# Layer 1 projections of a hybrid decoder step: the pages of cached keys are dealt to the units by kind, with weights 6, 3, 6, 6

## What is computed

```python
proj = _rmsnorm(x, norm_g) @ w_in                       # 1024 -> 4 * 1024 + 16
q, k, v, g, f = jnp.split(proj, [C_WIDTH, 2 * C_WIDTH, 3 * C_WIDTH, 4 * C_WIDTH], axis=-1)
q = _rmsnorm(q.reshape(Bn, L, C_HEADS, C_HEAD_DIM), q_g)
k = _rmsnorm(k.reshape(Bn, L, C_HEADS, C_HEAD_DIM), k_g)
v = v.reshape(Bn, L, C_HEADS, C_HEAD_DIM)
...
past_k = cache_k[page_table].reshape(Bs, -1, C_HEADS, C_HEAD_DIM)
...
s = jnp.einsum('bqhd,bkhd->bhqk', q, k_all).astype(jnp.float32) * ATTN_SCALE
```

## Time and profile before

| | us |
|---|---|
| median of 3 runs | 3198.45 |
| the runs | 3194.75 to 3200.6 |
| the profiled execution | 3206.94 |
| span of its instructions | 3205.4 |

### The profile page before, as it was taken

The page is one execution under the profiler, slowest core; times in us unless marked ns, Lnnn a source line. Parts: engine busy times, 40 slices in busy tenths (PEclk is TensorE's granted clock), DMA queues, the critical chain, the costliest instruction groups (busy, mean ns, idle before and its releaser), DMA issues. The chain is left out here.

```text
span 3205.4 us, 46935 instructions
## 1 busy us (share of the span) xinstructions
PE 2827.6 (88%) x17133; PEld 2246.4 (70%) x17133; DVE 1608.6 (50%) x2154; ACT 1024.0 (32%) x1721; POOL 1381.3 (43%) x986
## 2 busy tenths in 40 slices
PE   3887979695998999889999965999999999999999
PEld 2887868683774998879899963555555555554787
DVE  4222223234365678888555536455555555553432
ACT  4323132322245222212112211444454544544100
POOL 0000000001000477667888853777777777777000
PEclk9998989897998999989999986999999999999899
DMA  4101010104563688879777756977878878874532
GB/s 122 35 21 40 20 40 20 40 13 147 175 184 117 195 263 280 257 256 292 256 255 238 255 172 145 251 206 224 240 218 224 238 209 235 227 217 131 179 118 74
DMA packets 327904, 547.51 MB, mean 171 GB/s; under 512 B 76093, under 2 KB 220129, under 8 KB 319212
## 3 DMA queue, kind: packets, MB, share of 16 engines
q1 hardware_dynamic: 263564, 471.12, 50.0%
q10 hardware_dynamic: 61120, 58.83, 5.3%
q0 software_dynamic: 3008, 14.81, 1.3%
HBM read 449.58 MB, written 95.12 MB: 170 GB/s over the span
## 5 line engine op out<-in xcount | busy, mean ns | idle before, releaser
L1151 POOL TENSOR_TENSOR p_kp<-p_kp,p_qb 128x1024 f32<-128x1024 f32 x256 | 628.6, 2483 | 391.6 <-DMA p_kp<-in_cache_k_dram 313.3
L1997 POOL TENSOR_TENSOR at_acc<-at_acc,at_w 128x512 f32<-128x512 f32 (+3 forms) x576 | 644.8, 1119 | 231.1 <-ACT at_w L2125 165.4
L112 PE MATMUL p_pb<-p_w,x_xh 128*128 128x256 f32 x2048 | 595.0, 291 | 14.3 <-DVE p_w L1465 14.3
L2160 DVE TENSOR_REDUCE at_mx<-at_mx 128x1 f32<-128x512 f32 (+3 forms) x640 | 382.5, 608 | 425.7 <-PE at_mx L2032 312.0
L113 PE MATMUL p_pb<-p_w,x_xh 128*128 128x256 f32 x2048 | 582.3, 284 | 0.0
L114 PE MATMUL p_pb<-p_w,x_xl 128*128 128x256 f32 x2048 | 581.6, 284 | 0.0
L2125 ACT ACTIVATE at_w<-at_st,c_nckt 128x512 f32<-128x512 f32 (+3 forms) x640 | 389.5, 622 | 365.8 <-PE at_st L2058 193.4
L1567 DVE TENSOR_REDUCE p_sc<-p_kp 128x16 f32<-128x1024 f32 x256 | 308.2, 1215 | 230.6 <-POOL p_kp L1151 230.5
L112 PEld LDWEIGHTS p_pb<-p_w,x_xh 128*128 128x128 f32 x2048 | 393.6, 192 | 26.7 <-DVE p_w L1465 15.4
L113 PEld LDWEIGHTS p_pb<-p_w,x_xh 128*128 128x128 f32 x2048 | 395.5, 193 | 0.0
L114 PEld LDWEIGHTS p_pb<-p_w,x_xl 128*128 128x128 f32 x2048 | 394.6, 193 | 0.0
(11 more groups left out here) (296 smaller groups left out, 3837.2 us busy)
## 6 DMA issues: line engine op xcount, KB each, us to landing
p_kp<-in_cache_k_dram SPq DMA_DIRECT2D x256, 512.0 KB, 4.9
at_vp<-in_cache_v_dram SPq DMA_DIRECT2D x256, 512.0 KB, 5.4
o_mt<-mixed SPq DMA_DIRECT2D x32, 512.0 KB, 4.9
p_raw<-in_w_in_dram SPq DMA_DIRECT2D x32, 512.0 KB, 7.3
at_q<-qh SPq DMA_DIRECT2D x32, 512.0 KB, 10.7
at_k<-kh SPq DMA_DIRECT2D x32, 512.0 KB, 8.3
l_raw<-in_w_in_dram SPq DMA_DIRECT2D x20, 512.0 KB
mixed<-l_w POOLq DMA_DIRECT2D x8, 1028.0 KB, 4.2
```

What stands on the lines that cost most here:

```text
L112: nc.tensor.matmul(out, lhs[0], rhs[0], start=(k == 0), stop=False)
L1151: nc.gpsimd.tensor_tensor(kp[:, g % 4], kp[:, g % 4], qb[:], ALU.mult).then_inc(kmul, 1)
L1997: nc.gpsimd.tensor_tensor(t[:, 512 - wd:512], t[:, 512 - wd:512], W[n % RW][:, 0:wd], ALU.add).then_inc(accd, 1)
L2160: nc.vector.reduce_max(mx[:, u % 2, j, seg:seg + 1], MX[r % 2][:, 0:wd], AX.X).then_inc(mread, 1)
```

## The change

`keys_of` no longer deals the pages evenly. Each unit from 7 to 125 gets a weight by its kind, 6 for queries, values and gates and 3 for keys, and unit m gets the pages between the floors of the running sums' shares of 256. The first seven and the last two units still get none. Nothing else is changed; a keys unit now has one page or two, the others two or three.

```diff
     PAGES = B * z.PG
     FIRST = 7
+    SHARE = {"q": 6, "k": 3, "v": 6, "g": 6}
 
     def keys_of(m):
 
-        span = N - 2 - FIRST
-        lo, hi = ((max(0, min(span, x - FIRST)) * PAGES) // span for x in (m, m + 1))
+        share = [0] * FIRST + [SHARE[kind] for _, _, kind in UNITS[FIRST:N - 2]] + [0, 0]
+        lo, hi = (sum(share[0:x]) * PAGES // sum(share) for x in (m, m + 1))
         return range(lo, hi)
```

## The result

The changed kernel takes 3217.5 us in the median of 5 runs (3213.4 to 3220.0), against 3200.6 for the kernel before in the same comparison (5 runs, 3194.8 to 3205.0): a ratio of 1.0051, 95% interval 1.0037 to 1.0065, slower by some 17 us. Its profiled execution took 3217.5 us, like its median.

What follows compares the result with a forecast made beforehand. VectorE's queue was taken to pace the keys, the page loop values and gates; +12 - 45 + 52 - 11 = +8 us made 3215 us profiled, 3206.5 on the median's scale, range 3189 to 3223.

Steps and rivals of the forecast that it cites:

- Step A: Queries: nine more pages, between VectorE's sums alone (+5 us) and the page loop's pace (+14); taken as +12.
- Step B: Keys: 31 page sums fewer on VectorE and a shorter key gain, -45 us (-59 to -34).
- rival 1: Faster: queries' loop has room, VectorE drops below TensorE's pace in the keys; -13 us, 3185 us; chance 0.15.
- Step C: Values and gates: 21 more pages, each on the path at 2.5 us, +52 us (50 to 55).
- Rival 3: Added pages in values and gates hide behind the matmuls, only the keys' gain is left; -33 us, 3165 us; chance 0.05.
- Step D: Stage end: pages end last, so the stage closes some 7 us behind the last sum, not 18.5; -11 us.
- Rival 2: Clearly slower: keys' removed sums only uncover the VectorE-ScalarE chain, keys shrink by 34 only; +24 us, 3222 us; chance 0.12.
- Rival 4: No change: queries near their low end, keys a few us better, otherwise as forecast; -4 to +6 us; chance 0.28.
- three signs of being wrong: Values-and-gates page under 2.4 us; keys down to TensorE's pace; queries taking nine pages for nothing.

Runs made afterwards that it cites:

- the half product: Changed kernel, but GpSimd multiplies only half of each page's columns, so half the scores are left out: 3144.7 us, ratio 0.9831 to the kernel before.

## Why the prediction was right in its sign and half in its size

The forecast was +8 us, in a range of -9 to +25 against 3198.45; measured were +17. It came out toward the upper end of the +7 to +19 that the prediction gave its own steps. The direction and the mechanism hold; the size hangs in part on errors that cancelled. By its steps:

**Step A, queries, +12 forecast, +19 to +21 measured.** This is the term that was mis-sized most. The stretch from the earlier trace rows was right as a pace, but not what I made of it. The pages' tile before and after the one reload in the queries:

```profile
1088.00:1175.00 87.00, 0.00 (x0) 0.00 (x0) 37.48 (x32) 68.77 (x28) 1.00 0.84 276
1190.00:1268.00 78.00, 0.00 (x0) 0.00 (x0) 34.91 (x29) 70.74 (x30) 0.92 0.86 280
```

After the reload 29 pages took 78 us, 2.7 each as in the earlier trace rows. Before it the first four took their 9 us and the other 28 some 79, 2.8 each, because the loop starts empty: the fifth page's load can be issued only after the first sum. The reload held 11 us more, not 10. And I had taken 12 where the working gave 14, leaning towards VectorE as the bound; the half product shows that the loop was it. The range for the last query page, 1256 to 1265 us, missed 1268.

**Step B, keys, -45 forecast, -41 to -46 measured.** Right to a few us. VectorE's busy time came as described: 36 us of sums fewer and the gain at 1.10 us instead of 1.28, to 176 us where the working had 180. Its idle time of 32 us did not, and that the total of 29 was near it is luck: the waits for pages, reloads among them, fell to 14 us where the working had 24, and the waits for squares rose to 15 where it took 2 (in the second profile the two are 15 and 11 us). What I had not seen is that VectorE, once its arrears were made up, falls below TensorE's pace, so that the keys turn from VectorE's bound to TensorE's (200 busy of 208). That was rival 1's condition, and it came true without its gain, probably because the queries had left VectorE 20 us late (no run tests this alone).

**Step C, values and gates, +52 forecast, +45 to +48 measured.** Right in kind, 4 to 7 us too high: 21 pages at 2.1 to 2.3 us. The lower bound of 50 was too high, since two of the 155 pages lay multiplied when the stretch began: GpSimd has 153 products in it, 19 more than before and not 21, and is busy 371 us instead of 329. Idle it was 62 us instead of 56. Rival 3 is out by this.

**Step D, the close, -11 forecast, -7 to -13 measured.** The size is right, its reason only half: the pages do not end last. The last weights' low part,

```profile
1853.27 2.27 DVE L1466 TENSOR_TENSOR p_w<-p_raw,p_w 128x1024 fp32r<-128x1024 f32 x1
```

was followed by 54 us of pages, as worked out, but the gate rows' last store, issued at 1911.3, landed as the last, just as before: 3.65 us lie between that issue and the close in both profiles, while scores that end last close 3.7 us after the last sum, which would have been 1912.9. TensorE's last chunk began at 1858, some 2.5 us behind the low part, since its wait for the raw weights a unit earlier had put it back too. It was a tie that I decided for the wrong side, at 2 us.

The terms from the first profile of each kernel sum to 19 - 45 + 48 - 13 = 9 us, near the forecast's 8. That closeness is luck: 7 us too few in A stand against 4 too many in C and 2 too few saved in D. And that profile of before stood 6 to 9 us above its median, and I carried its difference over to after as if it were an offset of all profiles. It was not: after's profile stood at its own median. The rest of the miss lies there. The second profiles give +17 for the same four terms, with A at 21, B at -41, C at 45 and D at -7.

Of the rivals, none ended as the outcome. Rival 2 asked for keys that shrink by only 34; they did not. Rival 4, no change, is shut out by the interval. Of the prediction's own three signs of being wrong two came: a page in values and gates cost less than 2.4 us, and the keys came down to TensorE's pace. The scores' store was not the last of the stage either. What did come as written are the gain near 1.1 us, the 134 waits for products and TensorE's idling at the weights.

## What to carry to other kernels

Where a side loop (load, product, sum, slot freed) runs beside a main one, work out its own time for the whole stage first: as an estimate from the rows here, 252 pages at 2.6 us and seven reloads at 10 are 725 us, and what is left to the 801 of the three stretches before is idle time that a dealing can only move. Taking its work out of the stretch that looks worst then only makes the loop idle there, and the pages return at the loop's price, 2.1 to 2.3 us, where they had cost 1.3 to 1.7. What paid was to shorten the loop itself: the query row issued one wait earlier (-14 us), then the idle ends (a start at unit 3, more pages behind the last weights), some 36 us together.

Take a second profile, and the medians of several runs, before a term of a few us is read from the first: the same program's keys took 254 and 250 us, its close 18.5 and 12.4.

## What the runs showed of the hardware

The key gain, with both inputs in SBUF, takes 0.69 us alone. Its mean over the keys went with the products that it meets: 0.72 us beside half products, 1.10 with 39 pages, 1.28 and 1.40 in the two profiles of before with 69, 1.50 with 80. The Trainium skill ("SBUF — State Buffer", "Who interferes with whom") has such an operation and one of GpSimd's that reads SBUF exclude each other, and the trace agrees. The gain of 2.19 us in the earlier trace rows began at 1275.34, 0.7 us into this product of the kernel before,

```profile
1274.64 2.34 POOL L1151 TENSOR_TENSOR p_kp<-p_kp,p_qb 128x1024 f32<-128x1024 f32 x1 [0.27 <-DMA p_kp<-in_cache_k_dram]
```

and ended 0.55 us behind it, as if it had run only once the product was over; with GpSimd idle the next but one took 0.69. That the mean differed by 0.12 us between two profiles of one program says how much it hangs on where the loads happen to land.
